# Feed-forward inputs in three products of 256 columns, and a relaid launch

## The reference

```python
def first_block(x, p, positions, w_in_sb, w_out_sb, w_in_dil, w_out_dil, ...):
    cos, sin = rope_tables(positions)
    h = x
    for i in range(DEPTH):
        u = rms_norm(h, g_mix_pre[i])
        y = ...  # i == 0: stick_breaking_attention(u, ...), i == 1: dilated_attention(u, ..., cos, sin)
        h = h + rms_norm(y, g_mix_post[i])
        u = rms_norm(h, g_ffn_pre[i])
        f = jnp.square(jax.nn.relu(u @ w_ff_in[i])) @ w_ff_out[i]
        h = h + rms_norm(f, g_ffn_post[i])
        gate = jax.nn.sigmoid(rms_norm(h, g_ple[i]) @ w_ple_gate[i])
        h = h + (p[i] @ w_ple[i]) * gate
    return h
```

## Time and profile before

| | us |
|---|---|
| median of 3 runs | 1702.3 (1702.23 to 1706.57) |
| profiled execution | 1700.7 |
| its span in the profile | 1698.8 |
| TensorE busy | 1648.4 |
| VectorE busy | 1204.1 |
| ScalarE busy | 914.3 |

### The profile page before, as it was taken

One profiled execution on the slowest core, in us unless ns is written; L12 is line 12 of the kernel. 1 busy time (PEld: TensorE's weight loads), 2 busy tenths in 40 slices (PEclk: granted clock), 3 DMA queues, 4 the chain that ended last, 5 costly groups with the idle time before them and its releaser, 6 DMA issues.

```text
span 1698.8 us, 25392 instructions
## 1 busy us (share of the span) xinstructions
PE 1648.4 (97%) x10062; PEld 1413.4 (83%) x10062; DVE 1204.1 (71%) x1412; ACT 914.3 (54%) x1185; POOL 0.2 (0%) x4
## 2 busy tenths in 40 slices
PE   7999999999998999999999999999999999999998
PEld 6988888988887888899865778888888878789998
DVE  5866778778885878766578478876667666577754
ACT  5777664475337765467367453332234265565553
POOL 0000000000000000000000000000000000000000
PEclk9999999999999999999999999999999999999999
DMA  6834668745651566633130325456644432145652
GB/s 225 264 115 132 197 196 274 237 149 188 213 172 51 156 198 226 208 125 116 53 124 2 124 84 181 144 162 228 216 140 154 165 108 85 49 150 176 194 174 80
DMA packets 242824, 264.71 MB, mean 156 GB/s; under 512 B 7055, under 2 KB 223122, under 8 KB 242706
## 3 DMA queue, kind: packets, MB, share of 16 engines
q1 hardware_dynamic: 240780, 258.77, 47.0%
q10 hardware_dynamic: 1926, 4.32, 0.7%
HBM read 262.01 MB, written 1.05 MB: 155 GB/s over the span
## 4 chain that ended last, share of the span: by engine, by line
PE 78%; DVE 11%; ACT 8%; issue 2%; DMA 0%; ACTq 0%; DVEq 0%
PE ps L788 77%; DVE wlo L2107 3%; DVE y L2438 2%; ACT pr L2022 1%; ACT whi L1410 1%; DVE u L2545 1%; DVE pr L2727 1%; DVE y L2556 1%; PE ps L1303 1%; DVE qk L2290 0%; DVE qk L2288 0%; DVE work L2285 0%; ACT u L1619 0%; DVE small L2719 0%; ACT y L1885 0%
## 5 line engine op out<-in xcount | busy, mean ns | idle before, releaser
L788 PE MATMUL ps<-u,whi 128*128 128x256 f32 (+1 forms) x3544 | 872.6, 333 | 11.8 <-DVE u L2594 5.5
L788 PEld LDWEIGHTS ps<-u,whi 128*128 128x128 f32 x3544 | 599.2, 190 | 97.4 <-issue 14.0
L788 PE MATMUL ps<-u,wlo 128*128 128x256 f32 (+1 forms) x2052 | 629.0, 307 | 0.0
L2107 DVE TENSOR_TENSOR wlo<-raw,whi 128x2048 fp32r<-128x2048 f32 (+6 forms) x213 | 454.1, 2132 | 185.0 <-ACT whi L1410 175.8
L1410 ACT ACTIVATE whi<-raw 128x2048 fp32r<-128x2048 f32 (+6 forms) x213 | 381.0, 1789 | 195.4 <-PE ps L788 172.8
L788 PEld LDWEIGHTS ps<-u,wlo 128*128 128x128 f32 x2052 | 388.8, 189 | 19.5
L788 PE MATMUL ps<-hid,whi 128*128 128x512 f32 (+1 forms) x1212 | 352.7, 363 | 0.0
L788 PE MATMUL ps<-hid,wlo 128*128 128x256 f32 (+1 forms) x864 | 260.9, 302 | 0.0
L788 PEld LDWEIGHTS ps<-hid,whi 128*128 128x128 f32 x1212 | 216.2, 189 | 39.7 <-issue 3.4
L788 PEld LDWEIGHTS ps<-hid,wlo 128*128 128x128 f32 x864 | 163.1, 189 | 7.0
L2438 DVE SCALAR_TENSOR_TENSOR y<-idle_half,cc,y 128x1024 f32<-128x1024 f32 x70 | 89.9, 1285 | 5.0
(11 more groups left out here) (281 smaller groups left out, 1650.5 us busy)
## 6 DMA issues: line engine op xcount, KB each, us to landing
raw<-in_ffn_w_up SPq DMA_DIRECT2D x44, 1024.0 KB, 5.1
raw<-in_w_ff_in SPq DMA_DIRECT2D x32, 1024.0 KB, 5.4
raw<-in_w_ff_out SPq DMA_DIRECT2D x32, 1024.0 KB, 5.5
modw<-in_w_mod SPq DMA_DIRECT2D x112, 256.0 KB, 4.1
idle_half<-in_w_mod SPq DMA_DIRECT2D x80, 256.0 KB, 3.9
raw<-in_w_in_dil SPq DMA_DIRECT2D x18, 1024.0 KB, 5.2
raw<-in_w_in_sb SPq DMA_DIRECT2D x11, 1024.0 KB, 8.1
raw<-in_w_ple_gate SPq DMA_DIRECT2D x8, 1024.0 KB, 5.2
```

The costliest lines, as they stand in the source:

```text
L788: return pe.matmul(out_, lhsT, rhs, start=start, stop=stop, skip_group_check=True)
L2107: nc.vector.tensor_tensor(wlo[:, s % SPLIT, 0:n], raw[:, c["r"] % RAW, 0:n], whi[:, s % SPLIT, 0:n].bitcast(F32), ALU.subtract).then_inc(* ...
```

## The change

**Feed-forward inputs.** `paired` no longer holds for relu². The groups of `ff_in0` and `ff_in1` are made by three products of 256 columns in one sum. VectorE's relu reads that sum from PSUM itself, once the chunk's products are done, and frees the banks (`normed`).

**Launch.** x is transposed into four banks of its own, and x times gain is split straight from them, with no root in it: gain alone is transposed and moved ahead. Sums of squares are made within `stick_v`; its values get the root as a factor when ScalarE reads them out, and queries and keys get it from VectorE, which reads the groups of `stick_qk` in a new `stick_scaled`, in place of ScalarE's copies. The two products of 512 on the constant are gone. The angles (and the conditioning after them) move from the launch to behind chunk 1.

**Modulation.** Tiles are dealt out by vector, and by another table; the sets' products move from chunks 13, 42, 60, 72 to 24, 38, 61, 91 (the last set's stay at 101).

**Rotation.** In `dil_qk0` to `dil_qk2` VectorE rotates a group's pending tile ahead of the next remainder of weights, not behind it; and the dilated softmax ends up behind `mod_kept`.

```diff
-        share = dict(stick_qk=1, stick_v=2, stick_out=1, ff_out0=2, dil_qk0=1, dil_v0=1, dil_qk1=1, dil_v1=1,
-                     dil_qk2=1, ff_out1=2, up00=4, down00=4, up01=4, down01=4)
+        share = dict(stick_v=2, stick_qk=2, stick_out=1, ff_in0=1, ff_out0=2, dil_v0=1, dil_v1=1, ff_in1=1, ff_out1=2, up00=4, down00=4, up01=4, down01=4)
...
-            if p["T"] != S or p["evac"] not in ("y", "relu2", "gated") or p["name"] == "dil_out":
+            if p["T"] != S or p["evac"] not in ("y", "gated") or p["name"] == "dil_out":
...
-        VREADS = {"gate", "relu2", "y", "gated", "gated2", "conv", "poolw"}
+        VREADS = {"qk1", "gate", "relu2", "y", "gated", "gated2", "conv", "poolw"}
...
+                    group_sem[g[0]["gi"]] = "normed" if p["evac"] == "relu2" else "group_read_v" if p["evac"] in VREADS else "group_read_s"
...
-                sp.dma_start(squares[:, :, :], A["const_squares"].rearrange("p (j c) -> p j c", j=8)).then_inc(loaded["squares"], 16)
-                sp.dma_start(freq[:, :], A["const_freq"]).then_inc(loaded["freq"], 16)
-                sp.dma_start(posi[:, :], A["positions"].to_broadcast([P, S])).then_inc(loaded["pos"], 16)
+                sp.dma_start(squares[:, 0:2, :], A["const_squares"][:, 0:2 * P].rearrange("p (j c) -> p j c", j=2)).then_inc(loaded["ident"], 16)
...
-                        if p["name"] == "stick_v":
-                            context_turned(2 * g + c["k"] // 4)
+                        if p["name"] == "stick_v" and g == 0:
+                            if not c["first"]:
+                                square_sums(1, 0)
+                                square_sums(1, 1)
+                                pe.wait_ge(loaded["rows"], 16 * 12)
+                                pe.transpose(ps[:, 5, S:S + at_row], rows[0:at_row, 0, :], ident[0:at_row, 0:at_row]).then_inc(*up("turned", "rows"))
+                                pe.wait_ge(*at("normed", ("x", 3)))
+                        if p["name"] == "stick_v" and g == 1:
+                            if c["first"]:
+                                square_sums(1, 2)
+                                square_sums(1, 3)
+                            else:
+                                pe.wait_ge(*at("moved", "rows"))
+                                root_turned(1)
+                                pe.wait_ge(loaded["squares"], 16)
+                            for q in () if c["first"] else (2, 3, 0, 1):
+                                if q == 0:
+                                    pe.wait_ge(*at("rstd_ready", 1))
+                                if q == 1:
+                                    pe.wait_ge(*at("turned_copied", (1, "root")))
+                                context_turned(q)
...
+                    for k in range(KD):
+                        for t in range(2):
+                            last = pe.transpose(launch_tile(k)[:, t * P:(t + 1) * P], xin[:, t, k * P:(k + 1) * P], ident)
+                        if k % 2:
+                            last.then_inc(*up("turned", ("x", k // 2)))
...
-                    for b in (6, 7):
-                        mm(ps[:, b, :], ones, squares[:, 0:4, :].rearrange("p j c -> p (j c)"), True, True)
...
+                    for k in range(KD):
+                        if k == 4:
+                            split_high(0)
+                        act.wait_ge(*at("turned", ("x", k // 2)))
+                        act.wait_ge(*own())
+                        nc.scalar.activation(uh[:, k, 0:S], launch_tile(k), ACT.Copy, scale=gain(phases[2], k)).then_inc(
+                            *up("operand_high", (2, k)))
+                    split_high(1)
...
+                    dve.wait_ge(*at("weights_used", grp[-1]["s"]))
                     dve.wait_ge(*own())
                     nc.vector.scalar_tensor_tensor(yy, A_, 0.0, root_wide(2), ALU.max, ALU.mult).then_inc(*up("normed", (i, g)))
...
+            def stick_scaled(p, g):
+
+                c = p["groups"][g][0]
+                dve.wait_ge(*at("weights_used", c["s"]))
+                dve.wait_ge(*own())
+                nc.vector.scalar_tensor_tensor(
+                    (k1 if g % 2 else q1)[:, g // 2 * 2:g // 2 * 2 + 2, :], acc(c, S), 1.0 if g % 2 else HD ** -0.5, root_wide(2), ALU.mult, ALU.mult).then_inc(
+                    *up("group_read_v", ("group", c["gi"])))
+
             def stick_projections(p):
 
                 for g, grp in enumerate(p["groups"]):
                     c = grp[0]
+                    if g >= 1:
+                        stick_scaled(p, g - 1)
                     if g >= 3:
                         stick_mask(2 * g - 6)
                         stick_mask(2 * g - 5)
@@ -2484,6 +2567,7 @@
                         stick_low(g - 4)
                     mod_keep(c["r"] - 3)
                     mod_scaled(c["r"])
+                stick_scaled(p, len(p["groups"]) - 1)
...
+                    dve.wait_ge(*at("moved", "gain"))
+                    for k in range(KD):
+                        if k == 4:
+                            split_low(0)
+                        dve.wait_ge(*at("operand_high", (2, k // 2 * 2 + 1)))
                         dve.wait_ge(*own())
-                        nc.vector.tensor_scalar(lnv[:, 0:S], ang[:, :], 1 / (2 * np.pi), off, ALU.mult, ALU.add).then_inc(
-                            *up("vector_step"))
+                        nc.vector.scalar_tensor_tensor(ul[:, k, 0:S], launch_tile(k), gain(phases[2], k), uh[:, k, 0:S].bitcast(F32), ALU.mult, ALU.subtract).then_inc(
+                            *up("operand_low", (2, k)))
+                    split_low(1)
...
+                        if p["evac"] == "qk2" and (p["name"] != "dil_qk0" or g > 1):
+                            rotate_pending()
                         if grp[-1]["s"] + SPLIT not in early + late + behind_tail(p):
                             split_low(grp[-1]["s"] + SPLIT)
+                        if grp[-1]["r"] == 1:
+                            angles()
+                            conditioning()
```

More of the change, by code:

```diff
@@ new lines, in _ @@
+                    act.wait_ge(*at("turned", "rows"))
+                    act.wait_ge(*own())
+                    nc.scalar.activation(vec[:, 16:at_row], ps[:, 5, S + 16:S + at_row], ACT.Copy).then_inc(*up("moved", "rows"))
+                    act.wait_ge(*at("stat_summed", (1, 3)))
+                    act.wait_ge(*own())
+                    nc.scalar.activation(lnv[:, 0:S], ps[:, 4, 0:S], ACT.Ln, scale=1.0 / D, bias=small[:, 40:41]).then_inc(*up("scalar_step"))
+                    act.wait_ge(*own())
@@ L1847, in _ @@
                     s0 = p.get("s0", 0)
-                    for k in range(4 if i == 1 else p["n"]):
+                    for k in range(p["n"]):
                         if k >= 2:
@@ L1889, in _ @@
                             *up("operand_high", (i, k)))
-                    if i == 2:
-                        for s in range(1, SPLIT):
-                            split_high(s)
                 elif kind == "linear":
@@ L1901, in _ @@
                         if p["name"] == "dil_qk0" and grp[0]["g"] == 2:
[L1902 to L1905 removed]
+                            root_columns(p["sums"])
                         if p.get("stat") and grp[0]["g"] >= 1:
@@ L1933, in _ @@
                             heads[0] += 1
+                        if p["name"] == "ff_out0" and grp[0]["g"] == 1:
+                            angles()
                         mod_rows(grp[-1]["r"] - 1)
-                        if p["name"] == "stick_v":
-                            context_copied(2 * grp[0]["g"] + 1)
-                        if not already and grp[-1]["s"] + SPLIT not in early + late:
+                        if p["name"] == "stick_v" and grp[0]["g"] == 1:
+                            for q in (2, 3, 0, 1):
+                                context_copied(q)
+                        if not already and grp[-1]["s"] + SPLIT not in early + late and grp[-1]["s"] > 1:
                             split_high(grp[-1]["s"] + SPLIT)
@@ L2517, in _ @@
+                    split_low(1)
+                    for g in range(4):
                         dve.wait_ge(*own())
-                        nc.vector.tensor_scalar(lnv[:, 0:S], lnv[:, 0:S], magic, magic, ALU.add, ALU.subtract).then_inc(
-                            *up("vector_step"))
-                        dve.wait_ge(*own())
-                        nc.vector.scalar_tensor_tensor(t, lnv[:, 0:S], -c1, ang[:, :], ALU.mult, ALU.add).then_inc(
-                            *up("vector_step"))
@@ L2532, in _ @@
-                        dve.wait_ge(*own())
-                        nc.vector.tensor_scalar(t, t, -3.1415925, None, ALU.max).then_inc(*up("normed", "angles"))
-                elif kind == "stats" and i == 1:
-                    split_low(0)
+                        nc.vector.tensor_copy(h[:, 2 * g:2 * g + 2, 0:S], ps[:, (6, 7, 3, 2)[g], :].rearrange("p (k c) -> p k c", k=2)).then_inc(
```

(4 more changed lines are left out.)

227 lines of the change are left out of this document (116 added, 111 removed).

## The result

The changed kernel takes 1707.27 us in the median of 9 runs (1706.45 to 1708.3), the kernel before 1702.3 beside it: a ratio of 1.0029 with a 95% interval of [1.0019, 1.0039], 5.0 us slower. Measured again on another chip it is 1.0021 [1.0012, 1.003]. The forecast was 1707.8, +5.5, with 0.41 for slower by over 0.3%, 0.50 for the same and 0.09 for faster; the result lies on the edge between the first two.

A forecast was written before the change was run, and what follows sets the result against it. The prediction took TensorE, busy for 97% of the span of 1698.8 us, to bound the kernel. Its terms, +6.3 + 1.3 + 1.5 − 3.6 = +5.5, on 1702.3 gave 1707.8 us, with a range of 1700.5 to 1712.0.

The forecast's parts named there:

- Term 1: Feed-forward inputs: three products make each step 0.013 us longer, 0.21 us a chunk over 30 chunks, +6.3 us.
- The rule of the Trainium skill: Feed-forward inputs, rival: a fixed 2.5 ns per extra product, 1.2 us over 480 steps, total 1702.7; chance 0.08.
- the rows: Profile rows of `stick_qk` and `ff_in0`: 0.360 against 0.347 us a step, 13 ns more for three products.
- Term 2: Launch: a lead of 4.3 us is eaten by VectorE's queue, first scores at 58.95 against 57.62, +1.3 us.
- The two waits: Launch: TensorE waits for `stick_scaled`, 1.6 us at chunk 6 and about 4.1 us at the first scores.
- P: Launch: start of the first product on weights, taken as 16.2 against 22.80, bounds 15.4 to 17.7.
- the lead kept: Launch, rival: VectorE's queue is 4 us shorter, nothing of the 4.3 us is lost, total 1700.7; chance 0.14.
- The clock, +1.5: Behind the launch's stall of about 4 us: the lower granted clock costs +1.5 us, from 0 to 2.5.
- Term 3: Dilated part: waits of 1.55 and 0.74 go, 0.7 of the third and 0.6 of clock too, −3.6 us.
- the third wait: Dilated part, ahead of the scores at 496.31: 1.77 us on rotated `qk`, of which 1.05 is left.
- Costed at nothing: Sets' products moved among chunks, sines and tables in `ff_out0`, transfers of small inputs: no cost.
- The sum: Whole kernel: +6.3 + 1.3 + 1.5 − 3.6 = +5.5 us, on 1702.3 gives 1707.8.

The follow-up runs named there:

- The second experiment: Kernel before, with only the feed-forward inputs changed to three products of 256 and relu from PSUM: 1710.31 us, 1.0046 of the kernel before.
- the first experiment: Changed kernel with relu2 doubled again (one product of 512, one of 256, halves added): 1708.09 us, 1.0029 of the kernel before.
- The sixth experiment: Changed kernel with four tile operations moved from the first two groups of `stick_qk` to groups 3 to 6: 1699.53 us, 0.9974 of the kernel before.
- the third: Changed kernel with no tile operations in `stick_qk`, two in each chunk of `stick_out`: 1704.11 us, 1.0009 of the kernel before.
- the filler: Changed kernel with 32 unread products of 256 columns ahead of the first scores: 1704.39 us (1.0006 of the kernel before); again 1704.38 against the changed kernel's 1706.93.
- the fourth experiment: Changed kernel with the rotations of `dil_qk0` to `dil_qk2` behind the remainder of weights again: 1707.17 us, 1.0025 of the kernel before.
- the second kernel of the seventh experiment: Changed kernel, both feed-forward inputs doubled without tiles; tiles in later `stick_qk` groups, `gate0`, dilated projections, `dil_out`: 1712.18 us, 1.0047 of the kernel before.

## Why the prediction was right

**Term 1, +6.3.** Right in mechanism and size: 0.360 against 0.347 us a step, 0.21 a chunk, 30 chunks 6.4. The second experiment shows it by itself, 3.2 us for each feed-forward input. The rule of the Trainium skill ("TensorE: Matmul & The Clock Gate", section "Wait — 56ns, not 53.3ns?") would have given 1.2; the runs decide for the rows. What the term missed is a cost outside of the chunks it counted: more of the doubled chunks of `ff_out0` and `ff_out1` run at 0.353 us behind it, ten and six more than before, and at 0.0066 us a step that is +1.1 and +0.6. Term 1 had these parts at nothing. "TensorE has no wait there; I cost it at nothing" was right for the removed copies and additions as far as TensorE goes, but the removal was not free of effect: the first experiment shows that without it the new tiles would not fit.

**Term 2, +1.3.** The steps were right one by one. The two waits are 1.64 and 4.02 us, forecast at 1.6 and 4.1; the first scores come 42.38 us after P, forecast 42.75. What was off is P, 14.66 and not 16.2: the sum let the first weights land at 11.9, and ScalarE began on them at 10.37 already, with no wait, right behind its first four reads of x. The sum had taken over the issue at 2.1 from the kernel before; in the changed kernel two small transfers that stood ahead have moved behind, and it is at 1.2. So the term is −0.6. The sixth experiment, with the launch's lead kept, shows that VectorE's queue was the cause, and the third that the same work put into the wrong chunk costs there as well, 3.3 of the 5.5 us.

**The clock, +1.5.** 1 to 2 us, by the filler. The size was taken from another window and from another wait (1.77 us, not 4.02), so that it fits is in part luck. The way it was worked out, the missing share of the clock times the window, also gives more than what it costs in time: 0.24 × 7 = 1.7 us where the profiles differ by 1.1, and in the other profile of the changed kernel (granted clock 0.61) 0.39 × 7 = 2.7 where they differ by 2.0.

**Term 3, −3.6.** By the balance −3.2, and −0.8 of clock behind it: −4.0. The waits of 1.55 and 0.74 are gone, and 1.05 left of the third is 1.16. But the reason that was given for the second and third, the rotations' new place, doesn't hold for this kernel: the fourth experiment puts them back and nothing returns. Without the tiles VectorE is early enough in either order. With tiles there and the rotations ahead, in the second kernel of the seventh experiment, these waits stay away too, so each half of the change may be enough alone; tiles as many as before with the rotations ahead were not tried. And what is left of the third wait is ScalarE's reading of the values and not a rotation's step: there the number fits by luck.

**Costed at nothing.** The sets' products do cost the same in time of their own; but they interrupt the doubled steps, and what pace follows can change there.

**The sum.** −0.6 + 1.5 + 6.4 − 4.0 + 1.7 = +5.0, against +5.0 measured. That the forecast is within half a us of it owes something to two misses of opposite sign: the launch 1.9 better, the slower doubled steps 1.7 worse. Of the rivals, the lead kept didn't come true as the kernel stands, but did when four operations were moved.

## What to carry to other kernels

Work that nobody waits for yet can hold up a read of PSUM that somebody waits for in the same queue: a launch that was 6.7 us faster gave 6.1 of it back, and moving four operations to groups 3 to 6 made the kernel 0.26% faster than the one before the change. Where two parts of a change look separable, add up the queue of the engine that both load: the three products cost TensorE 0.21 us a chunk and save VectorE 0.79, and only with them does a tile operation fit. A place for such work is to be tried chunk by chunk, since `stick_out` and `gate0` gave back 3.3 and 4.5 us where later groups of `stick_qk` gave back nothing.

## What the runs showed of the hardware

- A step of one product of 512 and one of 256 columns in fp32r has two paces, 0.347 and 0.353 us, with the same instructions and the same granted clock. In these profiles a pace changed only where something else was issued between steps or TensorE waited, and it was the same in both profiles of a kernel. Three products of 256 showed only 0.360. The Trainium skill ("TensorE: Matmul & The Clock Gate", section "Wait — 56ns, not 53.3ns?") has N ÷ 2.4 GHz and 2.5 ns for each product, which is 0.320 us for 768 columns and 2.5 ns for each; the steps have 13.3 ns for each product at the faster pace and at three products.
- A standstill of 4.0 us was followed by a granted clock of 0.76 over 7 us in one profile and 0.61 in the other, and with the standstill filled it was 1.00 in both. A similar stretch in code that no kernel here changes (0.66 over 10 us, 1.8 us of time) was there in some profiles and not in others.
